# Scan stage of a hybrid encoder layer: two heads' key products as 64-row pairs, gate columns turned between the last token tiles, activation table sets chosen by hand

## The reference

```python
def _wkv7_step(state, inp):
    r, w, k, v, a, b = inp
    sa = jnp.einsum('phvk,phk->phv', state, a)
    state = state * w[:, :, None, :] + sa[..., None] * b[:, :, None, :] + v[..., None] * k[:, :, None, :]
    return state, jnp.einsum('phvk,phk->phv', state, r)

    # mlstm_mixer
    gates = (gates + gate_b).reshape(bn, sn, 2, 2, M_HEADS)
    ig = _flip_bwd(jnp.moveaxis(gates[:, :, 0], 2, 0))
    lf = _flip_bwd(jnp.moveaxis(jax.nn.log_sigmoid(gates[:, :, 1]), 2, 0))

    # around them
    groups = jnp.concatenate([y_g.astype(x.dtype), y_r.astype(x.dtype), y_m.astype(x.dtype)], axis=-1)
    mix = jnp.einsum('bsc,cd->bsd', groups, w_out[l])
    x = _layer_norm(DEEPNORM_ALPHA * x + mix, ln1_g[l], ln1_b[l])
    ffn = _moe(x, router_w[l], router_b[l], exp_w1[l], exp_b1[l], exp_w2[l], exp_b2[l])
    x = _layer_norm(DEEPNORM_ALPHA * x + ffn, ln2_g[l], ln2_b[l])
```

## Time and profile before

| | |
|---|---|
| median of three runs | 1296.55 us (1292.99 to 1297.01) |
| profiled execution | 1295.78 us |
| its span, first to last instruction | 1294.0 us |
| mean granted clock of TensorE | 0.985 of full speed |
| PE busy | 1218.9 us (94%) |
| DVE busy | 308.0 us (24%) |
| ACT busy | 328.3 us (25%) |
| GpSimd busy | 27.8 us (2%) |
| table loads on ACT, inside the expert loop | 64, of 1283 ns each |
| moved from memory | 428.36 MB, 332 GB/s over the span |

### The profile page before, as it was taken

The page is one execution under the profiler, slowest core; times in us unless marked ns, Lnnn a source line. Parts: engine busy times, 40 slices in busy tenths (PEclk is TensorE's granted clock), DMA queues, the critical chain, the costliest instruction groups (busy, mean ns, idle before and its releaser), DMA issues.

```text
span 1294.0 us, 15449 instructions
## 1 busy us (share of the span) xinstructions
PE 1218.9 (94%) x6275; PEld 570.2 (44%) x6275; DVE 308.0 (24%) x748; ACT 328.3 (25%) x520; POOL 27.8 (2%) x37
## 2 busy tenths in 40 slices
PE   7999999998899999999999999999999999999995
PEld 6875889895533333333333333333333333333331
DVE  1345857552511111111111111111111111111113
ACT  1333436343211212221221222121222121121122
POOL 1001010100000000000000000000000000000000
PEclk9999999998799999999999999999999999999998
DMA  9333000004969999999999999999999999999994
GB/s 334 135 111 136 1 1 1 2 1 195 396 268 407 428 429 427 428 429 403 406 429 428 430 429 429 428 426 427 428 430 428 429 429 428 426 429 429 429 429 206
DMA packets 42238, 429.80 MB, mean 332 GB/s; under 512 B 4844, under 2 KB 10035, under 8 KB 17507
## 3 DMA queue, kind: packets, MB, share of 16 engines
q1 hardware_dynamic: 40656, 427.56, 78.9%
q10 hardware_dynamic: 1267, 1.02, 0.4%
q0 software_dynamic: 288, 0.85, 0.2%
HBM read 428.36 MB, written 1.05 MB: 332 GB/s over the span
## 4 chain that ended last, share of the span: by engine, by line
PE 68%; DMA 22%; DVE 5%; ACT 3%; issue 1%; ACTq 0%; POOL 0%; SPq 0%; DVEq 0%
PE bank L1161 26%; DMA ring<-in_exp_w 22%; PE bank L1191 11%; PE bank L829 5%; PE bank L1133 3%; PE bank L839 3%; PE bank L999 2%; PE bank L985 2%; PE bank L998 2%; PE bank L1142 2%; PE bank L963 2%; PE bank L1081 2%; PE bank L1180 1%; DVE pool L1667 1%; DVE pool L1662 1%
## 5 line engine op out<-in xcount | busy, mean ns | idle before, releaser
L1161 PE MATMUL bank<-ring,pool 128*64 128x512 f32 x1280 | 288.7, 596 | 11.0 <-DMA ring<-in_exp_w 11.0
L1191 PE MATMUL bank<-ring,pool 128*64 128x512 f32 x1024 | 226.8, 595 | 0.0
L1161 PE MATMUL bank<-pool 128*64 128x512 f32 x768 | 174.6, 596 | 0.0
L1161 PEld LDWEIGHTS bank<-ring,pool 128*64 128x64 f32 x1280 | 87.9, 137 | 194.1 <-issue 170.9
L1191 PEld LDWEIGHTS bank<-ring,pool 128*64 128x64 f32 x1024 | 70.6, 137 | 154.0 <-issue 154.0
L1648 DVE TENSOR_SCALAR pool<-pool 128x128 f32<-128x128 f32 x64 | 19.3, 344 | 420.6 <-PE bank L1161 420.6
L1660 DVE TENSOR_SCALAR pool<-bank 128x512 f32<-128x512 f32 x32 | 22.1, 692 | 330.7 <-PE bank L1161 330.7
L1161 PEld LDWEIGHTS bank<-pool 128*64 128x64 f32 x768 | 51.9, 136 | 106.6 <-issue 106.6
L784 ACT ACTIVATE pool<-bank 128x512 f32<-128x512 f32 x32 | 19.1, 598 | 250.4 <-PE bank L1191 250.4
L774 ACT ACTIVATE pool<-bank 128x256 f32<-128x256 f32 x32 | 12.3, 385 | 237.3 <-PE bank L1173 237.3
L1133 PE MATMUL bank<-pool 64*128 64x512 f32 x264 | 65.6, 614 | 0.7 <-ACT pool L784 0.7
(11 more groups left out here) (282 smaller groups left out, 1078.5 us busy)
## 6 DMA issues: line engine op xcount, KB each, us to landing
ring<-in_exp_w SPq DMA_DIRECT2D x144, 2048.0 KB, 20.8
pool<-in_exp_w SPq DMA_DIRECT2D x48, 2048.0 KB, 24.9
ring<-in_w_in SPq DMA_DIRECT2D x4, 2048.0 KB, 9.3
ring<-in_w_out SPq DMA_DIRECT2D x2, 2048.0 KB, 7.8
ring<-in_w_in SPq DMA_DIRECT2D x2, 1536.0 KB, 13.5
pool<-in_consts SPq DMA_DIRECT2D x1, 1665.0 KB, 19.7
ring<-in_w_in SPq DMA_DIRECT2D x1, 1632.0 KB, 6.6
pool<-in_x SPq DMA_DIRECT2D x1, 1024.0 KB, 5.5
```

What stands on the lines that cost most here:

```text
L1161: last = mm(bank[4 + g][hp, :], lhs, w[:, k % 2, o:o + 512], start=False, stop=(k == KD - 1))
L1191: last = mm(bank[6][SLOTS * hf:SLOTS * hf + SLOTS, :], hT[:, k % 4, SLOTS * (k // 4):SLOTS * (k // 4) + SLOTS], w2s[k // 4][:, k % 4, 512 ...
```

## The change

Three parts.

*Key products.* `ktz` and `btz` (a copy for each head, the other half zeroed) give way to one `kt` and one `bt` with both heads' halves. The product of head 0 takes partitions 0 to 63 of both operands and that of head 1 partitions 64 to 127, and the two are issued alternately, chunk by chunk. The products stay the same, in the same banks and order. DVE makes two operands in place of four; PE turns two blocks for each direction in place of four, and ACT copies them out in one instruction of 256 columns in place of two of 128.

*Gate columns.* The eight transposes that turn the gate columns stand between `tok_tile(4)` and `tok_tile(5)`, and no longer behind both. Since `tok_tile(5)` still reads the turned input, the rows that DVE makes from the gate columns no longer lie in its place: `row0`, `row2` and `row3` lie in `o_grp` and `row1` in slot 5 of `ring`.

*Table sets.* Six `preload_act_table_set` calls name the set to hold. One set with both Ln and Exp is held through the scans and the norms, one with Sigmoid through the expert loop; the set with Ln and Exp is named once more ahead of the last norm.

```diff
-        row0 = view(o_xT, 2, S)
-        row1 = view(o_xT + 512, 2, S)
-        row2 = view(o_xT + 1024, 2, S)
-        row3 = view(o_xT + 1536, 2, S)
+        row0 = view(o_grp, 2, S)
+        row1 = rview(5, 3072, 2, S)
+        row2 = view(o_grp + 512, 2, S)
+        row3 = view(o_grp + 1024, 2, S)
...
-        ktz = [rview(5, 2048 + 512 * h, 2, NCH, P) for h in range(2)]
-        btz = [rview(5, 3072 + 512 * h, 2, NCH, P) for h in range(2)]
+        kt = rview(5, 2048, 2, NCH, P)
+        bt = rview(5, 2560, 2, NCH, P)
...
+            nc.scalar.preload_act_table_set("sigmoid_and_others")
             for i in range(NR):
                 base_of(i)
...
+            nc.scalar.preload_act_table_set("natural_log_exp_and_others")
             act.wait_ge(s_kk2, 1)
             key_scales(0)
             decay_exps(0)
             for j in (4, 5):
                 act.wait_ge(s_proj, NT + j + 1)
                 A(gel[:, j - 4], bank[(NT + j) % 4][:, 0:512], ACT.Gelu).then_inc(s_base, 1)
+            nc.scalar.preload_act_table_set("natural_log_exp_and_others")
             act.wait_ge(s_grow, 1)
...
-                    for h in range(2):
-                        hc = slice(HD * h, HD * h + HD)
-                        last = A(bktok[:, d, :, hc], pview(4 * d + 2, 0, 2, 2, P)[:, :, h, hc], ACT.Copy)
-                    last.then_inc(s_bkev, 1)
+                    A(bktok[:, d], pview(4 * d + 2, 0, 2, P), ACT.Copy).then_inc(s_bkev, 1)
...
+            nc.scalar.preload_act_table_set("sigmoid_and_others")
             act.wait_ge(s_gath, 1)
...
+            nc.scalar.preload_act_table_set("natural_log_exp_and_others")
             wide_root(3)
             wide_root(4)
...
-            for j in range(6):
+            for j in range(5):
                 tok_tile(j)
...
             last.then_inc(s_gtr, 1)
+            tok_tile(5)
...
-                for n, (d, f, b) in enumerate(FILLS):
-                    h = f % 2
-                    if f == 1:
+                for n in range(0, len(FILLS), 2):
+                    d, f, _ = FILLS[n]
+                    if f == 0:
                         pe.wait_ge(s_prev, 8 * pt + 1 + 2 * d)
                     for c in range(NCH):
-                        last = mm(pview(4 * d + b, 0, 2, 256)[:, c], (ktz, btz)[f // 2][h][:, d, c],
-                                  ar[:, d, c].rearrange("p a t -> p (a t)"), start=True, stop=True)
-                    last.then_inc(s_prod, 1)
-                    if n == 3 and pt:
+                        for h in range(2):
+                            hp = slice(HD * h, HD * h + HD)
+                            last = mm(pview(4 * d + FILLS[n + h][2], 0, 2, 256)[:, c], (kt, bt)[f // 2][hp, d, c],
+                                      ar[hp, d, c].rearrange("p a t -> p (a t)"), start=True, stop=True)
+                            if c == 1:
+                                last.then_inc(s_prod, 1)
+                    if n == 2 and pt:
                         scans_turned(pt - 1)
                 for d in range(2):
                     pe.wait_ge(s_prev, 8 * pt + 5 + 2 * d)
-                    for h in range(2):
-                        tr(pview(4 * d + 2, 0, 2, 2, P)[:, 0, h], btz[h][:, d, d], ident)
-                        last = tr(pview(4 * d + 2, 0, 2, 2, P)[:, 1, h], ktz[h][:, d, d], ident)
-                    last.then_inc(s_bk, 1)
+                    tr(pview(4 * d + 2, 0, 2, P)[:, 0], bt[:, d, d], ident)
+                    tr(pview(4 * d + 2, 0, 2, P)[:, 1], kt[:, d, d], ident).then_inc(s_bk, 1)
...
-                for h in range(2):
-                    own_half = hsel[:, h:h + 1]
-                    V.scalar_tensor_tensor(ktz[h], by_chunk(kdir), own_half, by_chunk(e_inv), ALU.mult, ALU.mult)
-                    V.scalar_tensor_tensor(btz[h], by_chunk(tmpk), own_half, by_chunk(e_inv), ALU.mult, ALU.mult)
+                V.tensor_tensor(kt, by_chunk(kdir), by_chunk(e_inv), ALU.mult)
+                V.tensor_tensor(bt, by_chunk(tmpk), by_chunk(e_inv), ALU.mult)
...
             dve.wait_ge(s_gtr, 1)
+            dve.wait_ge(s_qk, 1)
             dve.wait_ge(s_small, 64)
```

## The result

| | before | changed |
|---|---|---|
| median of 4 runs each, same chip | 1294.77 us (1291.58 to 1297.01) | 1280.66 us (1279.27 to 1282.13) |
| ratio changed / before, 95% interval | | 0.9883 [0.9863, 0.9903] |
| span of the profiled execution | 1294.0 us | 1278.3 us |
| mean granted clock | 0.985 | 0.987 |

The kernel became faster by 14.1 us, 1.2%. The forecast was 1283.5 us with a range of 1277 to 1290.5. By the spans the gain is 15.7 us. The prediction's rule was that it comes ahead of the first expert. So I read the same views again in the same order: the page's GB/s row, the chain that ended last (start us, us, what), and SP's queue (start us, us, engine, line, operation, out<-in, count).

A forecast was written before the change was run, and what follows sets the result against it. The start of the expert weight stream, set by the path before the first expert, was taken to bound the end. Terms of -15.25 and +2.4 for the clock gave -12.9, 1283.5 us taken, range 1277 to 1290.5.

The forecast's parts named there:

- The prediction's rule: Whole kernel: each microsecond saved before the first expert counts in full, the expert loop nothing, the last norm in full.
- Rival 4: Scans: idle PE in every pass keeps the clock at half through the levels, so slower, 1310 us; chance 0.04.
- Rival 3: Expert stream: its start does not move the end, only the last norm's -1 is left, 1295.5 us; chance 0.06.
- Entry, -1.9: Start of the scans: PE's idle time ahead of the first product shrinks from 2.6 to about 0.7 us.
- Key products, -4.2: Start of each pass: level 0 comes 1.0 us earlier, 2.2 in the first pass, as GpSimd ends hardly earlier.
- The clock, +2.4: Behind the new key products: PE's scattered idle brings a 1.6 us low-clock stretch in half of the passes.
- First-pass load, -1.2: First pass, between level 1 and the decay factors' mask: removing a 1.28 us table load gains nearly all of it.
- Rival 1: Scans: clock stays low for two stretches behind every set of products, costing 9.6 instead of 2.4; 1291 us, chance 0.13.
- End of the third pass, -2.55 and -2.7: Ahead of the second step: two loads' wait of PE goes (-2.55), and the low clock behind it (-2.7).
- First norm, -1.7: First norm: DVE no longer waits for ACT's table loads, 0.5 us for one half and 1.2 for the other.
- rival 2: Clock gives more: router's matmuls up to 3 us sooner, scattered idle free, 2.4 more; 1278 us, chance 0.15.
- Last norm, -1.0: Last norm: DVE's wait of 0.54 us for ACT, once for each half, goes.

The follow-up runs named there:

- loop_loads_back: Changed kernel without the table set named ahead of the expert loop, so its 64 loads return; 1280.63 us.
- the early products: Changed kernel with the wait for the last token tile's read moved from the first product to the first one writing that bank; 1279.02 us.
- the pairs alone: Kernel before with only the 64-row key products, their operands, transposes and copies changed; 1291.4 us, ratio 0.9968.
- the halves in turn: Changed kernel with both chunks of head 0 issued before both of head 1, not alternately; 1278.7 us.
- the two loads: Changed kernel with two table loads put back ahead of the Ln in the last pass's recurrence; 1286.14 us.
- the last comparison: Changed kernel run again, unchanged, as the base for two later runs on the same chip; 1279.58 us beside 1295.45 for the kernel before.
- the gate columns' turn alone: Kernel before with only the gate columns' transposes moved between the last two token tiles; 1291.09 us, ratio 0.9955.
- level 0 in halves: Changed kernel with GpSimd's second direction on DVE, first products ahead of the last Gelu, and level 0's first direction ahead of the keys' transposes; 1278.25 us.

## Why the prediction was right

**The rule held.** The first expert moved by 14.6 us, the first wait for weights by 14.5, the last norm by 1.0, and the span by 15.7. Rival 4 is out, since the two low stretches between the first product and the output products are 6.8 us in all, and not 30. Rival 3 is out: everything that was gained ahead of the loop arrived at the end. The loop's loads were worth nothing, as loop_loads_back shows: 41.1 us of loads ahead of one activation became 41.3 us of waiting.

**Entry, -1.9.** Measured -1.93, and what is late next is the Gelu, as said: taking the wait for it away (the early products) leaves no idle time at all.

**Key products, -4.2.** Measured -2.18 in the first pass and -1.02 in the second; the third gave -0.60, with a low stretch in it. That it is 1.0 and not the 3.2 by which PE's products are shorter is shown from two sides: the pairs alone give the same T+8.28, and less work on GpSimd brings level 0's first half to T+7.39. The rule of the Trainium skill, "TensorEngine Tiling (Array Packing)", section PSUM Bottleneck, that tiling doesn't speed up what evacuates PSUM, has the right direction: a mask of DVE takes 0.69 us before and 0.68 after. The eight of them end at T+8.0 before, when PE fed them one by one, and at T+6.0 after, 4.88 us in a row, while PE's products end at T+4.3. So it isn't they that end last either, but GpSimd at T+7.7. By the 2x of its section Theoretical Speedup alone the term would be some 10 us, an estimate from 6.92 us of products a pass. The traces have less: 4.31 us against 7.17 for 32 products in one piece at full clock, 1.7x. And the passes gained 1.0 each all the same.

**The clock, +2.4.** It is the one term that the traces can't hold against a number: the price of a stretch, 1.5 us, was right, the frequency behind the products was set too high (0.3 a pass, some 1.3 us in three passes), and low stretches come elsewhere too: one of before's, at 200, has no counterpart after (-1.65 from level 0 of the second pass to the third), and one of after's, at 136, none before. The forecast took stretches as added by the products; which of them would have come in any case, these runs can't say. Rival 1, two stretches on end behind every set of products, was in no trace.

**First-pass load, -1.2.** The table has +0.32 us there, because the changed kernel has a low stretch at 136 in that piece and before had its own ahead of level 0. So both pieces must be taken together, from the first product to the second pass, and traces with the same number of low stretches compared. With one stretch: 62.28 us before, and 60.20 to 60.26 in the four traces with the stretch behind the first products (the loop's loads back, the halves in turn, the two loads, and the changed kernel in the last comparison); where it falls at 136, as in the changed kernel's first trace, it is 60.42 to 60.44. That is -1.9 to -2.1 for pairs and load, where the terms without the clock have 1.0 + 1.2. With two stretches: 62.66 in the pairs alone, so 61.2 for one, and 60.2 with the sets too: the load is worth 1.0. With none: 60.94 in the gate columns' turn alone, against an estimated 58.7 for the changed kernel (60.2 less 1.5): -2.2 for both. The term was right within 0.3 us.

**End of the third pass, -2.55 and -2.7.** Measured -4.47 with a low stretch in the piece, and -5.5 without one (51.81 us in three of the traces), against -5.25. Putting two loads back cost 2.57 us of waiting on the path, and one low stretch of 1.53 us in place of two. In the three kernels that kept the wait (before, pairs alone, gates alone) two stretches followed on end, in the one that got it back a single one: the clock's part of this term is thus worth between 1.5 and 3.

**First norm, -1.7.** The part that the norm has in the -2.98 is 1.68. The rest, 1.33 us, was not in the sum: the router's matmuls take 4.90 us where they took 6.23. That is rival 2's first half, for which I had 3 us at most. The windows over just these matmuls, of the kernel before and of the changed one, have the clock at 0.57 and 0.73:

```profile
351.69:357.92 6.23, 6.23 (x11) 2.65 (x11) 3.10 (x17) 0.54 (x2) 0.00 (x0) 0.57 0.99 423
338.36:343.26 4.90, 4.90 (x11) 2.15 (x11) 3.10 (x17) 1.82 (x3) 0.00 (x0) 0.73 1.01 428
```

By the clock records the low time through norm and router lasts 17.1 us (340.0 to 357.0) in the three kernels without the table sets, and 13.7 us (327.4 to 341.0 in the changed kernel) in all ten with them. Two of the ten (the two loads back, and level 0 in halves) have 6.30 and 6.13 us in the router all the same, at 0.57 and 0.58: their low time starts later against these matmuls. So the clock comes back sooner, but what that is worth in the router differs from one execution to the next. No experiment was made on it.

**Last norm, -1.0.** Measured -1.0. The two halves, changed kernel's timeline, have no bracket where the earlier trace rows has 0.54:

```profile
1269.74 1.28 DVE L1574 SCALAR_TENSOR_TENSOR pool<-pool 128x1024 f32<-128x1024 f32 x1
...
1274.02 1.28 DVE L1574 SCALAR_TENSOR_TENSOR pool<-pool 128x1024 f32<-128x1024 f32 x1
```

**Taken together.** The sum was -12.9, the spans have -15.7. The 2.8 us between them are 1.65 for before's stretch at 200, 1.3 in the router and 0.1 in the projections; against them stand 0.3, since the changed kernel's two low stretches cost 2.7 (0.4, 1.5 and 0.8 in three lines of the table above) where I had 2.4. All but 0.1 are the clock's. The term that was off is thus the clock's, by its size: low stretches that fall otherwise from one execution to the next, 1.5 us each. The medians, -14.1, stand nearer to the forecast's -13.05 (1283.5 less 1296.55), and that is partly luck: with its fourth run the median of before is 1294.77 and not 1296.55. In the last comparison the medians have -15.9 (1279.58 beside 1295.45), which is what the spans say.

**No drain.** The Trainium skill, "ScalarE: Activation LUTs", section What ACT_TABLE_LOAD costs, adds 1380 ns of drain to a switch. By that the two loads put back at the end of the third pass would have cost 5.3 us of waiting; the timeline has 2 x 1.28 and a wait of 2.46 ahead of PE, and the path got 2.57 us longer. The trace disagrees with the drain here.

## What to carry to other kernels

When a change halves one engine's work, follow the two engines behind it, operation by operation, before counting the gain: here 3.2 us of PE a pass became 1.0, since GpSimd ended last. A saving on an engine that waits in every round, however large (82 us here), is waiting time of the same size; the few table loads that stood ahead of a wait of PE were worth more than all the others. And where idle time is removed or made on PE, read the granted clock behind it, in several executions: a low stretch costs as much as a typical term of such a sum.

## What the runs showed of the hardware

Products of 64 rows by two halves of the array run at once whether the instructions alternate between the halves or not: 32 of 256 columns in fp32 took 4.31 us alternating and 4.32 in pairs.

DVE and GpSimd hold each other up when both read two operands from SBUF: 0.69 became 1.63 us and 1.27 became 1.61 on 128x512 fp32, for the operation that started second, in six of six passes. So DVE's share of GpSimd's work ended 0.9 us later than by its own duration alone. With one operand of DVE in PSUM neither changed (0.68 and 1.27 us).

The clock's low stretches, at half speed and 3.4 us long each, came behind PE's scattered idle pieces of at most 1.4 us in 7 of 24 passes, behind a wait of 2.5 us in all four kernels that had it, and also where PE had been busy throughout (134 to 136 in the changed kernel).
